# First attention: a head's high and low query parts stacked on 128 rows, two score products a block instead of three

## What is computed

```python
q = rmsnorm_2(q.reshape(B, S, A_HEADS, A_HEAD_DIM), q_gain)
k = rmsnorm_2(k.reshape(B, S, A_KV_HEADS, A_HEAD_DIM), k_gain)
q = q.reshape(B, nb, BLOCK, A_KV_HEADS, G, A_HEAD_DIM)
kb, vb = band(k, nb), band(v, nb)
scores = jnp.einsum('bnqkgd,bnskd->bnkgqs', q, kb).astype(jnp.float32) * scale
scores = scores + bias                      # relative position, 32 buckets
scores = jnp.where(valid[None, :, None, None], scores, NEG)
p = jnp.exp(scores - m)                     # m: the larger of the row's maximum and the sink
denom = jnp.sum(p, axis=-1, keepdims=True) + jnp.exp(sink - m)
o = jnp.einsum('bnkgqs,bnskd->bnqkgd', p / denom, vb)
```

## Time and profile before

| | us |
|---|---|
| median of 3 runs | 2744.52 |
| lowest and highest | 2743.29, 2746.59 |
| the profiled execution | 2747.77 |
| its span, first to last instruction | 2746.5 |
| TensorE's busy time | 2687.4 (98%) |
| VectorE, ScalarE, GpSimd | 1460.4, 972.0, 351.7 |
| mean granted TensorE clock | 0.990 of full speed |
| the 16 heads' scores | 1284.4 to 1401.5 us of the span |

### The profile page before, as it was taken

How to read it: one execution, slowest core, us unless ns; L and a number is a source line. 1 busy time by engine, 2 the same in 40 slices (tenths; PEclk the granted TensorE clock), 3 DMA queues, 4 the chain that set the end, 5 groups by cost and what they waited for, 6 DMA issues and landing times.

```text
span 2746.5 us, 32270 instructions
## 1 busy us (share of the span) xinstructions
PE 2687.4 (98%) x13231; PEld 2254.1 (82%) x13231; DVE 1460.4 (53%) x2293; ACT 972.0 (35%) x1603; POOL 351.7 (13%) x403
## 2 busy tenths in 40 slices
PE   8999999999999999999999999999999989999999
PEld 7798888888787888888888888888888788888887
DVE  6535556565667544555675343554444677543433
ACT  4334333333354212234553222332222477432221
POOL 2200000000022000004550000000000477300000
PEclk9999999999999999999999999999999999999999
DMA  4322224523132277737323233233222210223321
GB/s 141 107 92 77 92 95 146 184 87 101 62 119 92 78 93 82 106 105 110 100 68 121 93 99 101 86 99 108 92 92 77 64 32 32 92 92 100 100 90 64
DMA packets 281194, 258.99 MB, mean 94 GB/s; under 512 B 40516, under 2 KB 276055, under 8 KB 281047
## 3 DMA queue, kind: packets, MB, share of 16 engines
q1 hardware_dynamic: 280640, 256.79, 33.8%
q10 hardware_dynamic: 407, 0.14, 0.0%
HBM read 242.23 MB, written 14.68 MB: 94 GB/s over the span
## 4 chain that ended last, share of the span: by engine, by line
PE 84%; DVE 9%; ACT 5%; issue 1%; DMA 1%; SPq 1%; POOL 0%; ACTq 0%; DVEq 0%; POOLq 0%
PE bank L1102 27%; PE bank L1104 27%; PE bank L1103 27%; DVE Wl L1795 1%; PE bank L1254 1%; ACT Wh L1446 1%; DVE TMP L1871 1%; SPq L2504 1%; DVE TMP L1995 1%; DVE TMP L1992 1%; ACT TMP L1569 0%; DVE Pl L1783 0%; DMA RAW<-in_a_w_in 0%; PE bank L1305 0%; PE bank L1113 0%
## 5 line engine op out<-in xcount | busy, mean ns | idle before, releaser
L1102 PE MATMUL bank<-Hh,Wl 128*128 128x512 f32 x2144 | 844.7, 394 | 8.8 <-DVE Wl L1795 3.7
L1104 PE MATMUL bank<-Hh,Wh 128*128 128x512 f32 x2144 | 837.8, 391 | 0.0
L1103 PE MATMUL bank<-Hl,Wh 128*128 128x512 f32 x2144 | 837.7, 391 | 0.0
L1446 ACT ACTIVATE Wh<-RAW 128x1024 fp32r<-128x1024 f32 (+2 forms) x454 | 441.3, 1022 | 453.6 <-PE bank L1104 379.7
L1795 DVE TENSOR_TENSOR Wl<-RAW,Wh 128x1024 fp32r<-128x1024 f32 (+1 forms) x408 | 478.2, 1215 | 145.0 <-ACT Wh L1446 144.3
L1102 PEld LDWEIGHTS bank<-Hh,Wl 128*128 128x128 f32 x2144 | 403.8, 188 | 97.0 <-issue 4.8
L1102 PE MATMUL bank<-Ph,Wl 128*128 128x512 f32 x1200 | 472.1, 393 | 10.2 <-DVE Pl L1783 3.7
L1104 PEld LDWEIGHTS bank<-Hh,Wh 128*128 128x128 f32 x2144 | 403.8, 188 | 86.0
L1103 PEld LDWEIGHTS bank<-Hl,Wh 128*128 128x128 f32 x2144 | 404.2, 189 | 85.4 <-issue 1.7
L1104 PE MATMUL bank<-Ph,Wh 128*128 128x512 f32 x1200 | 468.6, 390 | 0.0
L1103 PE MATMUL bank<-Pl,Wh 128*128 128x512 f32 x1200 | 468.3, 390 | 0.0
(11 more groups left out here) (301 smaller groups left out, 2489.9 us busy)
## 6 DMA issues: line engine op xcount, KB each, us to landing
RAW<-in_ffn_wg SPq DMA_DIRECT2D x44, 1024.0 KB, 5.3
RAW<-in_ffn_wu SPq DMA_DIRECT2D x44, 1024.0 KB, 5.3
RAW<-in_ffn_wd SPq DMA_DIRECT2D x32, 1024.0 KB, 5.2
RAW<-in_w_up SPq DMA_DIRECT2D x22, 1024.0 KB, 5.1
RAW<-in_w_in SPq DMA_DIRECT2D x20, 1024.0 KB, 5.1
RAW<-in_ffn_wd SPq DMA_DIRECT2D x16, 768.0 KB, 4.4
bias_scratch<-M SPq DMA_DIRECT2D x16, 512.0 KB, 7.9
RAW<-in_w_down SPq DMA_DIRECT2D x8, 1024.0 KB, 5.3
```

The lines of the kernel that those rows point to most:

```text
L1102: mm(o, ll, rh, start=start, stop=False)
L1103: mm(o, lh, rl, start=False, stop=False)
L1104: return mm(o, lh, rh, start=False, stop=stop)
L1446: run(Wh[:, n % 3, x:y], RAW[:, n % 2, x:y], ACT.Copy).then_inc(*w_hi.up(("w_hi", n, i)))
```

## The change

A pair's two tiles no longer hold high parts and low parts, but one head each: `QT[c][0]` is the even head, with its high part on partitions 0 to 63 (where its values stand in the bank) and its low part on partitions 64 to 127; `QT[c][1]` is the odd head, with its high part on partitions 64 to 127 and its low part on 0 to 63. ScalarE writes the high parts in two instructions of 64 partitions, VectorE the low parts in two instructions of 64 partitions, each of which reads one half of the partitions and writes the other. The semaphore of each engine is raised by the second instruction.

A head's scores are then two products a block. The first takes the high part of the query (64 rows) and the low part of the keys. The second takes all 128 rows of the tile and all 128 rows of the keys' high part, which stand on both halves: it sums high by high and low by high in one product.

```diff
             elif kind == "a_scores":
                 h, = s
                 part = slice(64 * (h % 2), 64 * (h % 2) + 64)
-                qh, ql = QT[h // 2 % 4]
+                q = QT[h // 2 % 4][h % 2]
...
-                        ins = mm3(o[:, s0:s1], qh[part, qs], ql[part, qs], kh[part, ks], kl[part, ks], True, True)
+                        mm(o[:, s0:s1], q[part, qs], kl[part, ks], start=True, stop=False)
+                        ins = mm(o[:, s0:s1], q[:, qs], kh[:, ks], start=False, stop=True)
...
-                run(QT[c % 4][0], bank(("a_qt", g, hp)), ACT.Copy, scale=gq_a).then_inc(*pair_hi.up(("a_qT_hi", c)))
+                for x, part in enumerate((slice(0, 64), slice(64, 128))):
+                    ins = run(QT[c % 4][x][part, :], bank(("a_qt", g, hp))[part, :], ACT.Copy, scale=gq_a[part, :])
+                ins.then_inc(*pair_hi.up(("a_qT_hi", c)))
...
-                qh, ql = QT[c % 4]
+                low, high = slice(0, 64), slice(64, 128)
                 dve.wait_ge(*at(("a_qT_hi", c)))
-                stt(ql, bank(("a_qt", g, hp)), gq_a, f(qh), ALU.mult, ALU.subtract).then_inc(
-                    *pair_lo.up(("a_qT", c), free=("a_qt", g, hp)))
+                for q, part, other in zip(QT[c % 4], (low, high), (high, low)):
+                    ins = stt(q[other, :], bank(("a_qt", g, hp))[part, :], gq_a[part, :], f(q[part, :]), ALU.mult,
+                              ALU.subtract)
+                ins.then_inc(*pair_lo.up(("a_qT", c), free=("a_qt", g, hp)))
```

## The result

| | before | changed |
|---|---|---|
| median of 4 runs, us | 2745.56 | 2762.34 |
| ratio, 95% interval | | 1.0062 (1.0048 to 1.0077) |
| span of the profiled execution | 2746.5 | 2761.7 |

The changed kernel is slower by 16.8 us; forecast were 12.6, and 2757.1 us for the time, with a range to 2765. The time lies in the range, 5.2 us above the forecast, of which 1.0 is the kernel before, whose median was 2744.52 in the forecast and is 2745.56 here. Three of the four runs lie between 2761.6 and 2763.0, the fourth at 2771.7.

The account below looks back on a forecast made before the run. The prediction took TensorE as the bound, busy 2687.4 of 2746.5 us. Scores +9.3, split writes +1.3 and +2.3, less 0.3 given back, made +12.6 on 2744.5: 2757.1 us, range 2745 to 2765.

Parts of the forecast that it names:

- A product inside a head, and the switch: Scores on TensorE: 256 columns end 0.12 us apart unswitched; each change between 64 and 128 rows adds 0.19 us.
- The sum of +9.3 us: Scores of all 16 heads: 0.57 us more in each of 15 heads, 0.7 us more in head 0.
- The rival of the head's borders: Scores: only a head's borders cost, the seven inner switches nothing; 2739.9 or 2736.9 us, chance 0.11.
- the rival of one direction: Scores: inside a head only one switch direction costs; scores +0.3, total 2748.1 us; chance 0.09, shared with a smaller price.
- The split writes: Query turns: additional half copies delay head 0 by 1.3 us and groups 1 and 2 by 2.3 us together.
- the part given back: Turn of group 1: TensorE arrives later, so its wait for the normalised queries goes, -0.3 us.
- Group 3: Query turn of group 3: no query product follows, values and output projection cover the copies, at no cost.
- the prediction's last sentence: Sum wrong if TensorE newly waits for VectorE or GpSimd, or granted clock of heads 4 to 15 leaves 1.00.
- The clock: Half clock behind TensorE's waits at the turns: no term in the sum, 2 to 4 us in the range either side.
- The last rival: Query turns: half writes cost half, so 1.3 + 2.3 becomes about 0; 2753.5 us, no chance of its own given.
- its main case: Scores: every inner switch between 64 and 128 rows costs; 2751 to 2762 us, chance 0.68.
- the rival of more falls: TensorE's clock falls more often behind longer waits and pauses at switches; +2 to +9, 2759 to 2766 us, chance 0.12.

Follow-up runs that it names:

- e4_whole_writes: Changed kernel's scores with the kernel before's whole writes of the turned queries (scores not right, for time only); +10.2 us against before, ratio 1.0043.
- e1_full128: Changed kernel with the first product of each block also on all 128 rows; 2744.97 us against 2745.49 before, ratio 1.0001.
- e2_grouped: Changed kernel with each head's four products of 64 rows first, then its four of 128; +4.7 us against before, ratio 1.0019.
- e3_split_writes: Kernel before with only its two writes of the turned queries split by halves of the partitions; +11.3 us against before, ratio 1.0041.

## Why the prediction was right, and what was mis-sized

- **A product inside a head, and the switch: right.** 0.31 us for 256 columns at full clock, loads that start only when the product ahead is nearly out, no gap at the border behind the head. The sum of +9.3 us measured 9.3 in the changed profile (stage +14.0, waits +4.7, equal loss to the clock) and 9.9 in `e4_whole_writes`; that the first agrees to 0.1 us is luck, between two single executions. At half clock, too, switched products start 0.51 us apart, as taken. A load starts 0.31 us after the product ahead of it started, not 0.2: near that one's end, as at the border. The rival of the head's borders is out by the first timeline above, that of one direction by the same rows: both steps take 0.31. `e1_full128` and `e2_grouped` show the price for none and for two switches a head. (For the rival of one direction the products' sum comes to between -0.2 and +0.2 us, not +0.3; nothing hangs on it.)
- **The split writes: mechanism right, size wrong.** The step took "one more of each ahead of it", at 0.59 and 0.67 us, and 2 x 0.58 at groups 1 and 2: +3.3 with the part given back. Measured are +1.5 (2.58 - 1.13), +1.7 and +1.6, +1.4 at group 3, less the 0.3: 5.9. The durations came from copies that overlap; those of alternating halves don't, and that hits all four copies of a turn and not only the two that are new.
- **Group 3: wrong.** It is the wait for VectorE that the prediction's last sentence names as a sign against its sum. The prediction put it at nothing, since no query product follows there. The product of the output projection that does follow needs the bank in which the turned queries of the first pair stood, and VectorE frees it with that pair's last low part. Before (two rows, the first with both pairs' low parts), then changed:

```profile
1376.12 1.40 DVE L2130 SCALAR_TENSOR_TENSOR Pl<-bank,sm,Ph 128x512 fp32r<-128x512 f32 x2
...
1377.01 0.47 PE L1102 MATMUL bank<-Ph,Wl 128*128 128x512 f32 x1
...
1389.91 0.76 DVE L2135 SCALAR_TENSOR_TENSOR Pl<-bank,sm,Pl 64x512 fp32r<-64x512 f32 x1
...
1390.81 0.47 PE L1103 MATMUL bank<-Ph,Wl 128*128 128x512 f32 x1 [1.41 <-DVE Pl L2135]
```

In the changed kernel the product starts 0.14 us after the low part that frees its bank (1389.91 + 0.76 = 1390.67). Before, the first of the two low parts ended at 1376.12 + 0.74 = 1376.86, and the product started 0.15 us later: the cover was already used up, which the timeline would have told.

- **What is given back at group 1: right.** The turn of group 1 waits for nothing in the changed kernel. (The 1.2 us for L2123 in its list is the turn of group 0. It waited 2.50 in the profile before and 1.1 to 1.2 in all others without unread products, wherever the stage started; why, isn't shown.)
- **The clock: as taken in the first profile, not in others.** 5.1 us lost in both profiles, as the sum without a term has it; at one place for longer and at the other not at all. The second profile of the changed kernel lost 3.4 more, with a fall at 1345 to 1352 us, behind the turn of group 2, where the prediction wanted none; its median is 2.6 us further from before. For the changed kernel the range of 2 to 4 us either way held; `e1_full128` lost 8.6 more than before and `e3_split_writes` 5.1.
- The last rival, half writes at half the cost, is out: 0.68 us for 64 partitions where 128 had 0.69.
- **Which case came in.** The time of 2762.3 us lies at the upper edge of what the prediction gave to its main case (2751 to 2762) and inside what it gave to the rival of more falls (2759 to 2766), so the time alone doesn't tell them apart. The profiles do: every switch has its price, and the changed profile lost no more to the clock than the one before.

In all +12.6 were forecast. The writes were 2.6 too low; the other 1.6 of the 16.8 us are less than two sets of runs differ (16.8 and 19.4).

## What to carry to other kernels

Count what a TensorE instruction costs from its neighbours, not from the number of instructions: fewer products that change the row count at each step are dearer than more that don't, so if operands are stacked on 128 rows, give the other products of the group 128 rows as well. When a write is split, look for who waits behind it in that engine's order and whose bank it frees. Work taken from the engine at the bound makes it arrive sooner at what others prepare: with about 13 us less of work TensorE waits 3.7 us more. And a profile is one execution. The stage was 12.3 us shorter between two profiles and the kernel 4.3 us faster over all runs, so look at the clock and time of all runs before you take a profile's gain for the kernel's.

## What the runs showed of the hardware

- Going between a product with 64 rows and one with 128 costs 0.19 us at full clock (0.31 instead of 0.12) and 0.30 at half (0.51 instead of 0.21) for 256 columns, in either direction, at every switch seen, whether or not a wait stands there. The Trainium skill, TensorEngine Tiling (Array Packing), Key Properties, says that changing the mode drains the engine; the trace agrees in that each such change costs, and adds the price. From 96 to 128 rows costs nothing (0.12 us).
- ScalarE's and VectorE's instructions here (512 columns) on one half of the partitions overlap by 0.07 to 0.09 us with the next on the same half, and not at all with one on the other half: starts 0.59 against 0.68 to 0.71 us apart on ScalarE, 0.67 against 0.76 on VectorE.
- Half the partitions takes as long as all of them for the same columns, 0.68 against 0.69 us.
